# Attention probabilities transposed inside a projection unit, and value products three slots behind the scores

## What is computed

```
h = layer_norm(x) * (1 + scale) + shift
q, k, v, g_attn, u, g_pool = split(h @ w_in)
s = einsum(q, k) * 64**-0.5                       # chunks of 64 queries against at most 192 keys
m = maximum(max(s), sink)
p = exp(s - m); p = p / (sum(p) + exp(sink - m))
o_attn = einsum(p, v)
o_pool = trailing means of u over 2, 4, 8, 16 rows, minus u, times w_pool
mixed = concat(o_attn * silu(g_attn), o_pool * silu(g_pool))
y = mixed @ w_out
x = layer_norm(2**0.25 * x + gate * y) * ln_g + ln_b
```

## Time and profile before

| what | us |
|---|---|
| runs of the kernel before | 460.98, 463.56, 463.92 (median 463.56) |
| profiled execution, its own time | 460.57 |
| its span, from the first to the last instruction | 458.8 |
| PE busy | 428.0 (93%) |
| DVE busy | 281.1 (61%) |
| ACT busy | 129.6 (28%) |
| POOL busy | 118.3 (26%) |

### The profile page before, as it was taken

One profiled execution on the slowest core, in us unless ns is written; L12 is line 12 of the kernel. 1 busy time (PEld: TensorE's weight loads), 2 busy tenths in 40 slices (PEclk: granted clock), 3 DMA queues, 4 the chain that ended last, 5 costly groups with the idle time before them and its releaser, 6 DMA issues.

```text
span 458.8 us, 6622 instructions
## 1 busy us (share of the span) xinstructions
PE 428.0 (93%) x2598; PEld 369.8 (81%) x2598; DVE 281.1 (61%) x541; ACT 129.6 (28%) x307; POOL 118.3 (26%) x83
## 2 busy tenths in 40 slices
PE   3769879999999999999999999999998999999993
PEld 0466879898999998988988889898966778888883
DVE  3597995230126666536755653775556687888875
ACT  1558432112110001533433353333454100000000
POOL 0141334022222210264233122321032332333300
PEclk9789899999999999999999999999999999999997
DMA  8998600415310411201200110110605022222231
GB/s 302 417 420 338 230 0 1 164 66 212 121 40 18 128 47 46 53 7 46 53 3 9 46 50 7 47 29 25 155 36 184 1 91 91 93 92 93 91 119 65
DMA packets 22545, 46.30 MB, mean 101 GB/s; under 512 B 11089, under 2 KB 13649, under 8 KB 21202
## 3 DMA queue, kind: packets, MB, share of 16 engines
q1 hardware_dynamic: 22514, 45.88, 28.5%
HBM read 40.61 MB, written 6.17 MB: 102 GB/s over the span
## 4 chain that ended last, share of the span: by engine, by line
PE 77%; DVE 12%; ACT 5%; issue 3%; DMA 2%; POOL 0%; SPq 0%; DVEq 0%; ACTq 0%; POOLq 0%
PE proj_ps L590 14%; PE proj_ps L591 13%; PE proj_ps L592 13%; PE proj_ps L723 7%; PE proj_ps L725 7%; PE proj_ps L724 7%; PE s_ps L623 2%; PE t_ps L652 2%; PE s_ps L526 2%; PE t_ps L546 2%; DMA xs<-x_all 2%; DVE xnT L1001 2%; ACT Pb L873 1%; PE proj_ps L566 1%; DVE Pb L1139 1%
## 5 line engine op out<-in xcount | busy, mean ns | idle before, releaser
L590 PE MATMUL proj_ps<-h_hi,w_hi 128*128 128x384 f32 x400 | 139.2, 348 | 0.3 <-DVE rt L1036 0.3
L591 PE MATMUL proj_ps<-h_lo,w_hi 128*128 128x384 f32 x400 | 135.1, 338 | 0.0
L592 PE MATMUL proj_ps<-h_hi,w_lo 128*128 128x384 f32 x400 | 135.0, 338 | 0.0
L1269 POOL TENSOR_TENSOR w_lo<-w_raw,w_hi 128x1024 fp32r<-128x1024 f32 x16 | 41.4, 2588 | 152.4 <-ACT w_hi L819 152.4
L590 PEld LDWEIGHTS proj_ps<-h_hi,w_hi 128*128 128x128 f32 x400 | 75.6, 189 | 4.9 <-issue 2.2
L591 PEld LDWEIGHTS proj_ps<-h_lo,w_hi 128*128 128x128 f32 x400 | 75.8, 190 | 0.9
L592 PEld LDWEIGHTS proj_ps<-h_hi,w_lo 128*128 128x128 f32 x400 | 75.7, 189 | 0.0
L723 PE MATMUL proj_ps<-wo_hi,m_hi 128*128 128x512 f32 (+1 forms) x152 | 58.6, 386 | 1.5 <-DVE mixed L1063 1.5
L725 PE MATMUL proj_ps<-wo_hi,m_lo 128*128 128x512 f32 (+1 forms) x152 | 58.4, 384 | 0.0
L724 PE MATMUL proj_ps<-wo_lo,m_hi 128*128 128x512 f32 (+1 forms) x152 | 58.4, 384 | 0.0
L1058 DVE SCALAR_TENSOR_TENSOR mixed<-th,proj_ps 128x384 f32<-128x384 f32 x24 | 13.3, 553 | 51.2 <-ACT th L833 51.2
(11 more groups left out here) (153 smaller groups left out, 600.2 us busy)
## 6 DMA issues: line engine op xcount, KB each, us to landing
w_raw<-w_in SPq DMA_DIRECT2D x18, 512.0 KB, 4.9
wada<-w_ada SPq DMA_DIRECT2D x8, 1024.0 KB, 11.0
xs<-x_all SPq DMA_DIRECT2D x9, 512.0 KB, 8.7
xf<-x_all SPq DMA_DIRECT2D x9, 512.0 KB, 4.1
wada_late<-w_ada SPq DMA_DIRECT2D x2, 2048.0 KB, 7.5
y_out<-yr SPq DMA_DIRECT2D x8, 512.0 KB, 2.9
wo_raw<-w_out SPq DMA_DIRECT2D x4, 512.0 KB, 3.3
wo_rest<-w_out SPq DMA_DIRECT2D x4, 512.0 KB, 9.2
```

Of the source, the lines that this page charges most:

```text
L590: pe.matmul(bank[:, 0:CW], w_hi[:, w, k, :], hi, start=(k == 0), stop=False)
L591: pe.matmul(bank[:, 0:CW], w_hi[:, w, k, :], lo, start=False, stop=False)
L592: mm = pe.matmul(bank[:, 0:CW], w_lo[:, w, k, :], hi, start=False, stop=(k == KT - 1))
L1269: pool.tensor_tensor(w_lo[:, b % 2], w_raw[:, b % RAW], w_hi[:, b % 2].bitcast(F32), ALU.subtract).then_inc(wlo_done, 1)
```

## The change

`SLOTS` gets one slot more, slot 22, which falls behind output piece m = 4. A new table, `TRANSPOSED_IN`, gives for each place of slots 2 to 21 the step s - 2 (and unit 67 in place of unit 69 for slot 19). At those places the transposes of that step are issued inside the unit, behind its second k slice (k = 1), and in the output stage behind k = 1 of pieces m = 1 (both pieces' k = 1) and m = 3. TensorE's slot i is then `values(i - 3)` and `scores(i)`. ScalarE's and VectorE's slot i copy step i - 2 in place of i - 1, and VectorE mixes step i - 3 in place of i - 2. So the transposes of step s run in the unit ahead of slot s + 2, its copies in slot s + 2, its products in slot s + 3. No instruction is added or taken away.

```
-SLOTS = {PLACES[4 * s // 3]: [s] for s in range(NSTEP + 2)}
+SLOTS = {PLACES[4 * s // 3]: [s] for s in range(NSTEP + 3)}
+TRANSPOSED_IN = {LAST_PROJ if n == NU - 1 else n: s[0] - 2 for n, s in SLOTS.items() if 2 <= s[0] < NSTEP + 2}
+T_SLICE = 1
...
                         for k in slices:
+                            if k == T_SLICE + 1 and n in TRANSPOSED_IN:
+                                p_transposes(TRANSPOSED_IN[n])
...
             def slot(i):
-                if 0 <= i - 2 < NSTEP:
-                    values(i - 2)
-                if 0 <= i - 1 < NSTEP:
-                    p_transposes(i - 1)
+                if 0 <= i - 3 < NSTEP:
+                    values(i - 3)
                 if i < NSTEP:
                     scores(i)
...
                 output((0, 1), k)
+                if k == T_SLICE and NU + 1 in TRANSPOSED_IN:
+                    p_transposes(TRANSPOSED_IN[NU + 1])
...
                     output((m,), k)
+                    if k == T_SLICE and NU + m in TRANSPOSED_IN:
+                        p_transposes(TRANSPOSED_IN[NU + m])
```

ScalarE's slot, where the copies to PT1 now are those of step i - 2:

```
             def slot(i):
-                if 0 <= i - 1 < NSTEP:
+                if 0 <= i - 2 < NSTEP:
-                    act.wait_ge(t_done, i)
-                    if i >= 2:
-                        act.wait_ge(pv_done, i - 1)
+                    act.wait_ge(t_done, i - 1)
+                    if i >= 3:
+                        act.wait_ge(pv_done, i - 2)
```

And VectorE's, where the numbers of the waits below these lines shift in the same way:

```
             def slot(i):
-                if 0 <= i - 2 < NSTEP:
-                    mix(i - 2)
-                if 0 <= i - 1 < NSTEP and keys_of(i - 1)[1]:
+                if 0 <= i - 3 < NSTEP:
+                    mix(i - 3)
+                if 0 <= i - 2 < NSTEP and keys_of(i - 2)[1]:
```

More of the change, by code:

```diff
@@ L854, in slot @@
             def slot(i):
-                if 0 <= i - 1 < NSTEP:
-                    k1, _ = keys_of(i - 1)
-                    w = 512 if i - 1 < NQ else 256
-                    act.wait_ge(t_done, i)
-                    if i >= 2:
-                        act.wait_ge(pv_done, i - 1)
+                if 0 <= i - 2 < NSTEP:
+                    k1, _ = keys_of(i - 2)
+                    w = 512 if i - 2 < NQ else 256
+                    act.wait_ge(t_done, i - 1)
+                    if i >= 3:
+                        act.wait_ge(pv_done, i - 2)
                     act.activation(PT1[0:k1, 0:w], t_ps[0:k1, 0, 0:w], ACT.Copy).then_inc(pt1_done, 1)
@@ L1104, in slot @@
             def slot(i):
-                if 0 <= i - 2 < NSTEP:
-                    mix(i - 2)
-                if 0 <= i - 1 < NSTEP and keys_of(i - 1)[1]:
-                    k2 = keys_of(i - 1)[1]
-                    w = 512 if i - 1 < NQ else 256
-                    if i - 1 >= NQ:
+                if 0 <= i - 3 < NSTEP:
+                    mix(i - 3)
+                if 0 <= i - 2 < NSTEP and keys_of(i - 2)[1]:
+                    k2 = keys_of(i - 2)[1]
+                    w = 512 if i - 2 < NQ else 256
+                    if i - 2 >= NQ:
                         k2 = P
[L1112 to L1115, removed]
+                    dve.wait_ge(t_done, i - 1)
+                    if i >= 3:
+                        dve.wait_ge(pv_done, i - 2)
+                    if packed(i - 2):
                         dve.tensor_copy(PT2[0:QB, 0:256], t_ps[0:QB, 1, 0:256])
```

## The result

| what | before | after |
|---|---|---|
| median of 20 runs, us | 461.80 (460.57 to 464.27) | 463.33 (462.70 to 464.77) |
| ratio of the times | 1 | 1.0036, 95% interval 1.0025 to 1.0047 |
| profiled execution, own time, us | 460.57 | 463.45 |
| its span, us | 458.8 | 461.5 |
| first scores (slot 0) start, us | 176.84 | 177.43 |

What follows compares the result with a forecast made beforehand. TensorE's row of starts was taken as the bound in slots 4 to 9. Gains of 1.4 + 0.3 + 1.5 + 0.4 = 3.6 us against 4.5 us of waits gave 461.5, plus 1.7 for level 463.2 us, range 458.8 to 466.8.

Steps and rivals of the forecast that it cites:

- The level of a run: Whole kernel: runs lie 1.7 us above the profiled execution, lifting the forecast from 461.5 to 463.2 us.
- transposes out of a packed slot: TensorE's packed slots: taking the transposes out saves 0.80 us each, ends 0.70 and 0.90.
- six transposes in a unit: TensorE inside a unit: putting six transposes between its matmuls costs 0.69 us.
- waits for Pb that go: TensorE's transposes: four waits for the softmax's scaled probabilities (Pb) disappear, together 1.5 us gained.
- wait in unit 45: Transposes in unit 45 wait 0.9 us for VectorE's copy in slot 10, which stands behind the trailing means.
- wait in piece 3: Transposes in output piece 3 wait 1.7 us for VectorE's copy in slot 20, behind tile 0's passes.
- wait of the products behind piece 4: Products of step 19 behind output piece 4 wait 1.7 us for VectorE's copy in slot 21, behind tile 1's passes.
- the case of the copies in time: Rival, also called "the late copies don't decide": the 3.6 us gain stays, 458.6 us on the forecast's level; chance 0.15.
- the late copies don't decide: Rival: VectorE's copies come in time or TensorE makes the waits up later, so 3.6 us stay gained, 458.6 us; chance 0.15.
- Dear insertions: Rival: transposes inside a unit cost 0.99 us, not 0.69, over eighteen insertions 5.4 us: 468.6 us; chance 0.10.
- Late neighbours: Rival: five more pairs of slots at neighbouring units wait 0.9 us each, 4.5 us more: 467.7 us; chance 0.07.
- Free crossing: Rival: TensorE's step from products to scores takes 0.22 us, not 0.32, so 1.3 us less: 461.9 us; chance 0.10.

Runs made afterwards that it cites:

- one kernel with as long an idle time: Changed kernel with the transposes behind the fifth k slice (k = 4) of their unit or piece, not behind k = 1: ratio 0.9952 to the kernel before.
- the refilled kernel: Changed kernel with the scores of step 19 computed four times over, filling TensorE's idle time ahead of the outputs: ratio 1.0011 to the kernel before.
- the run that takes two of them away: Changed kernel with VectorE's slots 20, 21 and 22 ahead of the two passes over the tile, not behind them: ratio 0.9961 to the kernel before.
- the two fastest kernels: Changed kernel with transposes behind k = 4 and VectorE's slots 20 to 22 ahead of the passes, without and with step 19's scores computed four times: ratios 0.9917, 0.9904.
- the kernel before with less work: Kernel before without three of four transposes of step 18 and half the products of step 17 in slot 19: ratio 1.0022 to the kernel before.

## Why the prediction was right or wrong

Within 1% had the largest chance and is what came, 1.5 us by the medians against the 0.9 us in the sum. But the predicted time, 463.2 us, which is almost the median of after, is right for wrong reasons, and it lies below the 463.56 shown of before, which would say slightly faster. Two steps failed.

- **The level of a run** failed: "the mean of the four times shown 462.26, 1.7 above the profiled one". Over 20 runs before's median is 461.80, 1.2 above its profiled execution, and after's profiled execution (463.45) is 0.1 above its median. Four times with a spread of 3 us didn't fix the level, the distance from the profiled execution wasn't the same in the two kernels, and this error hid the next one. A part of the spread has a place: the first scores start up to 1.1 us apart. The rest of the 3.7 us between the fastest and the slowest execution of before (460.57 and 464.27) was never profiled, and stays open.
- **The clock's term was missing.** "those whose transposes lie between unit 60 and the first output piece are hidden before and after, because TensorE idles 1.50 us ahead of that piece anyway": hidden, yes, but taking work out of the covered stretch made the idle time 0.58 us longer, and the first outputs ran at 0.62 of the clock, 1.58 us more for twelve matmuls (4.42 - 2.84). I had asked what work beside an idle time costs, and not what its absence does. Runs that fill the idle time, repeat the kernel or make the same idle time without the change bear it out; one kernel with as long an idle time kept the clock in its profiled execution.

By the terms:

| term | predicted, us | measured, us |
|---|---|---|
| transposes out of a packed slot | -0.80 | -0.80 |
| six transposes in a unit | +0.69 | +0.67 |
| products to scores | 0.32 | 0.32 |
| waits for Pb that go | -1.5 | -1.5 (all four gone) |
| wait in unit 45 | +0.9 | +0.85 |
| waits for the copy of step 18, ahead of the outputs' 13th matmul | +0.2 | hidden by the clock; 0.3 in the refilled kernel |
| wait in piece 3 | +1.7 | +1.61 |
| wait of the products behind piece 4 | +1.7 | +1.63 |
| slower outputs at the lower clock | none | +1.58 (1.15 net of the wait it hides) |

To the outputs the prediction's terms make 1.4 + 0.3 + 1.5 + 1.02 + 0.58 - 0.9 = 3.9 us gained (the fourth and fifth are what moves into the covered stretch: the products of step 15 and the transposes of step 16), and 4.16 were measured. Behind, they make 0.61 + 0.58 + 0.2 + 1.7 + 1.7 = 4.8 us lost, and 6.27 were measured. The same by the heads of the pieces: from pieces 0 and 1 to piece 2 12.43 us before and 14.00 after (+1.57, the clock; the transposes of step 18 come in there and those of step 19 go out, some 0.4 each), from piece 2 to piece 4 12.03 and 14.28 (+2.25, the wait and the transposes), from piece 4 to piece 5 5.72 and 8.12 (+2.40, the wait and the products). From piece 5 on the two are alike. Net 2.1 us in the profiled executions, where the sum had 0.9. The medians give 1.5, which leaves some 0.6 us. The fastest executions of the two kernels (460.57 and 462.70) are 2.1 us apart, as the profiles are; before's median is 1.2 above its fastest execution, after's 0.6. So the rest lies in how the executions spread, whose cause is open. A clock that held in some executions of after would fit too, but the mean clocks of its 32 executions, above, speak against it.

One comparison in the prediction is slightly off: the case of the copies in time, at 458.6 us, is said to lie in the range, which starts at 458.8.

The rivals: "the late copies don't decide" fell with the run that takes two of them away and gains 3.4 us. Dear insertions fell with the 0.67 us. Late neighbours fell with the list of waits, where unit 45 has the only wait for a copy among the units. Free crossing fell with the step of 0.32 us. It was the case of the Trainium skill, "TensorE: Matmul & The Clock Gate", Part 2, Step-by-step (the next weights are pulled in ahead): by that alone the step would be 0.22 us as between two pairs of products. The trace differs at the two changes from one division of the array to another that the rows show, 0.27 us from a unit to products and 0.32 from products to scores. It agrees where none is changed: whole-array transposes in a stream of whole-array matmuls start after a plain step of 0.18 us.

## What to carry to other kernels

When work is moved so that it depends on another engine's earlier step, look at what that engine has queued ahead of the step, not at how busy it is: VectorE was idle for 39% of the span and still 0.9, 1.6 and 1.6 us late, and putting its copies ahead of the passes over a tile turned 0.4% slower into 0.4% faster. Idle time that hides work can be worth leaving filled: ahead of a dense stage, count what is left in it, and read the granted clock just behind it. And where kernels differ by less than 1%, compare stretches of the profile and look at each execution's clock; one profile tells what can happen, not how often.

## What the runs showed of the hardware that was not expected

With 2.05 to 2.08 us of idle time ahead of the outputs, and only small matmuls in the last microsecond before it, the granted clock behind it was 0.50 to 0.65 over about 4.4 us in six of seven profiled executions, and 1.00 in the seventh, whose TensorE program up to there was the same as in one of the six. With 0.45 to 1.50 us it was 1.00 in all six executions. The price between profiled executions was 1.15 us (after against its refilled form), 1.49 (the two fastest kernels) and 2.65 (the kernel before with less work); between the medians it was 0.9, 0.5 and 1.1. What decides in a single execution, and how idle time and small matmuls share in it, stays open.
